# Attention stage of a streaming encoder layer: two key duplicates, one rope-key copy and the sums of the memory's squares are put in other slots

## The chip, the cores and the metric

One NeuronCore of a Trainium2 chip runs the kernel. The metric is the device time of one execution in microseconds (us). The kernel before took 849.5 us as the median of 3 runs (849.47 to 849.58).

## The reference, cut to what matters

One encoder layer is computed for 512 prompt tokens and 64 sample tokens (576 columns, `T`), float32. The input is normed and projected; two groups of 8 heads attend side by side; each group's output is normed, joined and projected by `w_o`; then come a cross-attention with 4 heads into 256 memory tokens, and a SwiGLU.

```python
h = rms_norm(x, g_mix)
fox_q, fox_k, fox_v, logf, mla_q, ckv, kr = project_mixers(h, pos, w_in, ...)
fox_o = attend(fox_q, fox_k, fox_v, ..., cum, cum)        # heads 0 to 7, keys of 64 rows
mk, mv = mla_keys_values(ckv, kr, w_ukv)                  # kr: the shared rope keys, 32 rows
mla_o = attend(mla_q, mk, mv, ...)                        # heads 8 to 15
x = x + concat(rms_norm(fox_o), rms_norm(mla_o)) @ w_o
m = rms_norm(mem, g_mem_src)                              # needs the sum of squares of each memory token
mem_k, mem_v = m @ w_mk, m @ w_mv
```

## The kernel before, in words

Each float32 product is made of three products of rounded parts (L460 to L462: high by high, low by high, high by low). ScalarE (ACT) rounds an operand to its high part; the low part is the rest, made by GpSimd (POOL) for weights, queries and keys and by VectorE (DVE) for activations. SyncE (SP) starts all loads.

The attention stage is one order written out by hand, in slots `s` from 0 to 96. There are 16 heads with 5 blocks of queries each, so 80 ticks; tick s is block s % 5 of head s // 5. In slot s, TensorE (PE) makes the scores of tick s (`scores`), then a piece of other work (`filler`, the slots in `CHUNKS`: a projection, a transpose of reciprocals, part of `w_o`), then the transposes of the probabilities of tick s - 2 (`turn`). DVE makes the maximum of tick s (`maxima`, L1666), evicts the filler of slot s - 1 (`evicted`, L1698 to L1743) and, in even slots, copies the transposed probabilities of tick s - 3 (`turned_dve`, L1676). ACT makes the exponentials of tick s (`expo`, L1044) and in odd slots the other copies. PE must not start a filler before the filler two before it is evicted (`filler_bank`: two PSUM banks in turn, semaphore `s_fev`), nor scores s before exponentials s - 2 (`s_ex`).

Dictionaries say what each engine does besides in which slot. Those the change touches: `KEY_HI_AT` (ACT: the high part of head c's keys, `key_hi`), `KEY_DUP_AT` (DVE: `key_dup`, L1640, a copy of 64 x 832 from the keys `kt` into the other half of `k1`), `KEY_LO_AT` (POOL: `key_lo`, L2155), `KR_AT` (POOL: the rope keys put under the keys of r, a copy L2199 and a rest L2201; first needed in slot 40), and `SPLIT_AT` (ACT: `split(b)`, the high part of weight block b; POOL's `rest(b)`, L2114, has its own `REST_AT`). Keys 6 are used from slot 30, keys 7 from slot 35. The pieces of all the dictionaries stand in one queue per engine, in the order in which the loop writes them.

For the memory, ACT squares `memf` (128 x 8 x 256) into `msq` in two halves in slots 71 and 73; POOL adds the halves up in slot 75 (L2212: 1024, 512 and 256 elements wide), and PE needs the sum in slot 87 (`s_mmacc`). From slot 75 on DVE makes the low parts of the memory (`meml`, L1797), after ACT made the high parts (`memh`).

Of the kernel before, what the change touches and what calls it, by code (L numbers as in the profile page):

```python
# [10 lines left out]
ALU = mybir.AluOpType  # L11
# [76 lines left out]
def build(nc, i_, o_, cum_dram):  # L88
# [10 lines left out]
    whi, c = place("whi", [128, 3, WB], F32R, c)  # L99
# [125 lines left out]
    with ExitStack() as ctx:  # L225
# [20 lines left out]
        def need(eng, s, value, i=0, per=0):  # L246

            if isinstance(i, int):
                if value + per * i > 0:
                    eng.wait_ge(s, value + per * i)  # L250
            else:
                eng.wait_ge(s, i * per + value)
# [787 lines left out]
        def _(act):  # L1040
# [137 lines left out]
            def high(j):  # L1178
# [10 lines left out]
                else:  # L1189
                    if j == 1:  # L1190
# [5 lines left out]

            HIGH_AT = (26, 31, 41, 51, 71, 77, 83, 89)
            QUERY_HI_AT = {1: 2, 2: 3, 9: 4, 10: 5, 19: 6, 20: 7}
            KEY_HI_AT = {5: 2, 6: 3, 14: 4, 15: 5, 25: 6, 28: 7}
            SPLIT_AT = {2: 16, 4: 17, 8: 18, 13: 19, 18: 20, 23: 21, 36: 22, 46: 23, 52: 24, 59: 25, 68: 26, 74: 27, 82: 28, 86: 29,  # L1200
                        87: 30, 92: 31, 93: 32}
            for s in range(LAST + 1):
                if 3 <= s < TICKS + 3 and s % 2 == 1:
                    turned_act(s - 3)
                if s - 1 in CHUNKS:
                    n = nth(s - 1)
                    bank = 6 + n % 2
                    for p, at in enumerate(KP_AT):
                        if s - 1 in (at, at + 1):
                            half = s - 1 - at  # L1210
                            act.wait_ge(s_fdone, n + 1)
                            if half == 0:
                                for r in (2 * p % 4, 2 * p % 4 + 1):
                                    act.wait_ge(s_qk, (5 * r + 25) if p < 2 else (5 * H + 5 * r + 5))
                            for e in range(2):
                                activation(keys_of(k1[2 * p % 4 + e][0:64, :], half), ps[64 * e:64 * e + 64, bank, 0:HK])\
                                    .then_inc(s_khi, 1)
                for h, at in enumerate(UQ_AT):
                    if s == at + 2:
                        act.wait_ge(s_fev, nth(at + 1) + 1)  # L1220
                        activation(q1[h % 4][:, :], qf[h % 4][:, :]).then_inc(s_uqhi, 1)
                if s < TICKS:
                    expo(s)
                if s in QUERY_HI_AT:
                    query_hi(QUERY_HI_AT[s])
                if s in KEY_HI_AT:
                    key_hi(KEY_HI_AT[s])
                if s in HIGH_AT:
                    high(HIGH_AT.index(s))
                if s in SPLIT_AT:  # L1230
                    split(SPLIT_AT[s])
                if s == FC_AT + 3:
                    act.wait_ge(s_fev, nth(FC_AT) + 1)
                    deviation(small[:, S_COL:S_COL + 5], small[:, S_COL:S_COL + 5], 512).then_inc(s_lsd, 1)
                if s == 70:
                    act.wait_ge(s_mem, 32)
                if s == 88:
                    act.wait_ge(n_col, 2)
                    deviation(small[:, S_MCOL:S_MCOL + 2], ps[:, 4, 0:2], D).then_inc(n_sd, 1)
                if s == 94:  # L1240
                    act.wait_ge(n_col, 3)
                    deviation(small[:, S_COL:S_COL + 5], ps[:, 4, 0:5], 512).then_inc(n_sd, 1)
                if s in (71, 73):
                    k = 4 * (s // 2 - 35)
                    act.wait_ge(s_qk, 70)
                    activation(msq[:, k:k + 4, :].rearrange("p a b -> p (a b)"), memf[:, k:k + 4, :].rearrange("p a b -> p (a b)"),
                               ACT.Square).then_inc(s_mmact, 1)
                if 74 <= s < 82:
                    k = s - 74
                    activation(memh[:, k, :], memf[:, k, :], scale=gains[:, G_SRC + k:G_SRC + k + 1]).then_inc(s_mmact, 1)  # L1250
# [245 lines left out]
        def _(dve):  # L1496
# [253 lines left out]
            LOW_AT = (27, 32, 42, 52, 72, 78, 84, 90)  # L1750
            QUERY_DUP_AT = {1: 2, 2: 3, 9: 4, 10: 5, 19: 6, 20: 7}
            MEMORY_LO_AT = (75, 76, 77, 80, 81, 82, 83, 84)
            KEY_DUP_AT = {5: 2, 6: 3, 14: 4, 15: 5, 25: 6, 28: 7}
            for s in range(LAST + 1):
                if s < TICKS:
                    maxima(s)
                if s - 1 in CHUNKS:
                    evicted(s - 1)
                if 3 <= s < TICKS + 3 and s % 2 == 0:
                    turned_dve(s - 3)  # L1760
                if 14 <= s <= 84 and s % 10 == 4:
                    joined(s // 10 - 1)
                if s % 10 == 0 and 10 <= s <= 80:
                    p = s // 10 - 1
                    dve.wait_ge(s_ex, 10 * p + 10)
                    need(dve, s_rb, p - 1)
                    at = S_SUM + 10 * (p % 2)
                    v.reciprocal(small[:, S_RI[p % 2]:S_RI[p % 2] + 10], small[:, at:at + 10]).then_inc(s_ri, 1)
                if s in QUERY_DUP_AT:
                    query_dup(QUERY_DUP_AT[s])  # L1770
                if s in KEY_DUP_AT:
                    key_dup(KEY_DUP_AT[s])
                if s in LOW_AT:
                    j = LOW_AT.index(s)
                    dve.wait_ge(s_ohi, j + 1)
                    dve.wait_ge(s_osq, j + 1)
                    v.scalar_tensor_tensor(hlo[:, j, :], out_of(j), gain(G_OUT, j), f(hhi[:, j, :]),
                                           ALU.mult, ALU.subtract).then_inc(s_olo, 1)
                if s == FC_AT + 5:
                    dve.wait_ge(s_lsd, 2)  # L1780
                    v.reciprocal(small[:, S_RCC:S_RCC + 5], small[:, S_COL:S_COL + 5]).then_inc(s_frc, 1)
                if s == 89:
                    dve.wait_ge(n_sd, 2)
                    v.reciprocal(small[:, S_MRC:S_MRC + 2], small[:, S_MCOL:S_MCOL + 2]).then_inc(n_rc, 1)
                if s == 91:
                    dve.wait_ge(n_row, 2)
                    v.tensor_copy(rmem[:, :], ps[:, 5, 0:NM]).then_inc(n_rs, 1)
                if s in (92, 93):
                    dve.wait_ge(n_rs, 2)
                    memory_key(s - 92)  # L1790
                if s == 95:
                    dve.wait_ge(n_sd, 3)
                    v.reciprocal(small[:, S_RCC:S_RCC + 5], small[:, S_COL:S_COL + 5]).then_inc(n_rc, 1)
                if s in MEMORY_LO_AT:
                    k = MEMORY_LO_AT.index(s)
                    dve.wait_ge(s_mmact, 2 + k + 1)
                    v.scalar_tensor_tensor(meml[:, k, :], memf[:, k, :], gain(G_SRC, k), f(memh[:, k, :]),  # L1797
                                           ALU.mult, ALU.subtract).then_inc(s_mmlo, 1)
# [308 lines left out]
        def _(pool):  # L2107
# [41 lines left out]
            def key_lo(c):  # L2149

                a = half_a(c)
                if c in (0, 2, 4, 6):
                    pool.wait_ge(f_lo, {0: 15, 2: 18, 4: 20, 6: 22}[c])
                pool.wait_ge(x_khi, c + 1)
                g.tensor_tensor(k2[c % 4][a, :], kt[a, :], f(k1[c % 4][a, :]), ALU.subtract).then_inc(x_klo, 1)  # L2155
                pool.wait_ge(x_klo, c + 1)
# [9 lines left out]
                       87: 30, 92: 31, 93: 32}  # L2166
            HIGH_AT = (26, 31, 41, 51, 71, 77, 83, 89)
            QUERY_LO_AT = {1: 2, 2: 3, 9: 4, 10: 5, 19: 6, 20: 7}
            KEY_LO_AT = {5: 2, 6: 3, 14: 4, 15: 5, 25: 6, 28: 7}
            RB_BUILD = (12, 26, 31, 41, 51, 70, 76, 82)  # L2170
            KR_AT = (27, 32, 37, 42)
            for s in range(LAST + 1):
                if s in RB_BUILD:
                    p = RB_BUILD.index(s)
# [15 lines left out]
                if s in KR_AT:  # L2190
# [1 line left out]
                    if r == 0:  # L2192
                        pool.wait_ge(s_kr, 4)
                    pool.wait_ge(s_qk, 5 * r + 25)
                    if r >= 2:
                        pool.wait_ge(s_uqlo, r)
                    else:
                        pool.wait_ge(s_rb, {0: 2, 1: 3}[r])
                    g.tensor_copy(k1[r][64:128, :], krf[64:128, :]).then_inc(s_krc, 1)  # L2199
                    pool.wait_ge(s_krc, 2 * r + 1)  # L2200
                    g.tensor_tensor(k2[r][64:128, :], krf[64:128, :], f(k1[r][64:128, :]), ALU.subtract).then_inc(s_krc, 1)  # L2201
# [1 line left out]
                if s - 1 in HIGH_AT and s not in (HIGH_AT[0] + 1, HIGH_AT[4] + 1):  # L2203
# [1 line left out]
                    pool.wait_ge(s_osq, j + 1)  # L2205
                    need(pool, s_oacc, j - 1 if j < 4 else j - 2)
                    g.tensor_tensor(sqacc[:, 0:T], sqacc[:, 0:T], tmp2[:, j % 2, :], ALU.add).then_inc(s_oacc, 1)
                if s == 75:
                    pool.wait_ge(s_mmact, 2)
                    for k, n in enumerate((4, 2, 1)):  # L2210
                        need(pool, s_mmacc, k)
                        g.tensor_tensor(msq[:, 0:n, :], msq[:, 0:n, :], msq[:, n:2 * n, :], ALU.add).then_inc(s_mmacc, 1)  # L2212

            def memory_key_lo(m):
                pool.wait_ge(s_mkhi, m + 1)
# [389 lines left out]
```

## Time and profile before

| what | us |
|---|---|
| median of 3 runs | 849.5 |
| profiled execution | 848.79 |
| its span in the trace | 847.0 |
| PE busy | 815.0 (96%) |
| DVE busy | 541.0 (64%) |
| ACT busy | 398.0 (47%) |
| POOL busy | 363.8 (43%) |

The span is the time from the first to the last instruction of the profiled execution; the 1.8 us around it belong to the launch. Busy time is the union of an engine's instructions, and PE's is modelled at its ends. The attention stage lies between about 95 and 306 us of the span.

### The profile page before, as it was taken

Reading aid. Unit: us, or ns where it says so; the run is one execution under the profiler, and the core shown is the slowest. Engines: PE = TensorE matmul, PEld = TensorE weight load, DVE = VectorE, ACT = ScalarE, POOL = GpSimd, SP = SyncE. Lnnn points to the kernel's source line nnn. Section 1 sums busy time; section 2 is a strip of 40 time slices with the busy share of each in tenths; the row PEclk is TensorE's granted clock in tenths of the full one; section 3 lists DMA queues with packets and bytes.
Section 4 is the critical chain, followed back from the end, with each engine's and each line's share of the span. In section 5 each row is a group of like instructions: output and inputs, shape, how many; then the busy total and the mean of one; then the engine's idle time right before and its main releaser. Section 6 shows DMA issues by size and latency. Waiting matters only on the chain.

```text
span 847.0 us, 16025 instructions
## 1 busy us (share of the span) xinstructions
PE 815.0 (96%) x5913; PEld 768.8 (91%) x5913; DVE 541.0 (64%) x911; ACT 398.0 (47%) x735; POOL 363.8 (43%) x213
## 2 busy tenths in 40 slices
PE   6999999999999999998999999999999989999995
PEld 6987998778887899987899999999999989999995
DVE  6245365666667755557488998889999887211214
ACT  6443464565676425455354555555455564221210
POOL 2652864555326444732195333333333335433420
PEclk9999999999999999999999999999999999999998
DMA  7332422201123333340041332222222223232103
GB/s 258 100 110 83 153 90 65 60 3 36 32 76 137 125 101 108 112 130 26 1 141 60 101 100 99 93 77 82 95 99 99 99 87 101 87 87 81 58 1 112
DMA packets 26391, 75.49 MB, mean 89 GB/s; under 512 B 3024, under 2 KB 7448, under 8 KB 26200
## 3 DMA queue, kind: packets, MB, share of 16 engines
q1 hardware_dynamic: 26336, 74.74, 27.7%
q8 instruction: 37, 0.61, 0.3%
q14 instruction: 18, 0.15, 0.1%
HBM read 68.20 MB, written 6.53 MB: 88 GB/s over the span
## 4 chain that ended last, share of the span: by engine, by line
PE 85%; DVE 7%; issue 2%; POOL 2%; ACT 2%; DMA 1%; DVEq 0%; SPq 0%; ACTq 0%
PE ps L460 26%; PE ps L462 25%; PE ps L461 25%; PE ps L612 2%; PE ps L630 2%; POOL hf L2241 1%; PE ps L874 1%; PE ps L478 1%; DVE tf L1914 1%; PE ps L591 1%; PE ps L590 1%; POOL wlo L2236 1%; PE ps L596 1%; DVE tl L1918 1%; PE ps L859 0%
## 5 line engine op out<-in xcount | busy, mean ns | idle before, releaser
L460 PE MATMUL ps<-hhi,whi 128*128 128x288 f32 x896 | 269.8, 301 | 11.9 <-DVE hlo L1519 6.9
L461 PE MATMUL ps<-hhi,wlo 128*128 128x288 f32 x896 | 265.7, 297 | 0.0
L462 PE MATMUL ps<-hlo,whi 128*128 128x288 f32 x800 | 237.5, 297 | 0.0
L2114 POOL TENSOR_TENSOR wlo<-wraw,whi 128x1024 fp32r<-128x1024 f32 (+1 forms) x48 | 113.5, 2369 | 174.7 <-ACT whi L1044 174.4
L460 PEld LDWEIGHTS ps<-hhi,whi 128*128 128x128 f32 x896 | 169.8, 190 | 15.1 <-issue 10.3
L1044 ACT ACTIVATE whi<-wraw 128x1024 fp32r<-128x1024 f32 (+3 forms) x138 | 114.7, 838 | 135.8 <-PE ps L462 121.7
L461 PEld LDWEIGHTS ps<-hhi,wlo 128*128 128x128 f32 x896 | 169.5, 189 | 0.2
L462 PEld LDWEIGHTS ps<-hlo,whi 128*128 128x128 f32 x800 | 151.2, 189 | 0.0
L2260 POOL TENSOR_TENSOR wlo<-wraw,whi 128x512 fp32r<-128x512 f32 x60 | 78.8, 1327 | 150.4 <-ACT whi L1044 150.4
L462 PE MATMUL ps<-hidlo,whi 128*128 128x288 f32 x352 | 104.7, 297 | 0.0
L2274 POOL TENSOR_TENSOR wlo<-wraw,whi 128x1024 fp32r<-128x1024 f32 (+1 forms) x24 | 56.3, 2348 | 79.6 <-ACT whi L1044 79.6
L1666 DVE TENSOR_REDUCE small<-ps 128x1 f32<-128x128 f32 (+4 forms) x80 | 39.0, 487 | 56.0 <-PE ps L596 50.9
L462 PE MATMUL ps<-tl,whi 128*128 128x288 f32 x240 | 71.4, 297 | 0.0
L461 PE MATMUL ps<-th,wlo 128*128 128x288 f32 x240 | 71.3, 297 | 0.0
L460 PE MATMUL ps<-th,whi 128*128 128x288 f32 x240 | 70.9, 295 | 0.0
L1044 ACT ACTIVATE whi<-ss 128x512 fp32r<-128x512 f32 x61 | 38.4, 631 | 63.6 <-PE ps L462 35.4
L462 PEld LDWEIGHTS ps<-hidlo,whi 128*128 128x128 f32 x352 | 66.7, 189 | 0.0
L1044 ACT ACTIVATE probs<-ps,small 128x128 f32<-128x128 f32 (+4 forms) x80 | 41.9, 524 | 42.8 <-DVE small L1666 42.0
L2064 DVE TENSOR_TENSOR tmp<-ps,rstd 128x576 f32<-128x576 f32 (+1 forms) x9 | 6.2, 691 | 85.2 <-PE ps L462 85.2
L460 PE MATMUL ps<-hidhi,whi 128*128 128x288 f32 x192 | 57.6, 300 | 2.1 <-DVE hidlo L2047 2.1
L461 PE MATMUL ps<-hidhi,wlo 128*128 128x288 f32 x192 | 57.4, 299 | 0.0
L460 PEld LDWEIGHTS ps<-th,whi 128*128 128x128 f32 x240 | 45.2, 188 | 0.0
(287 smaller groups left out, 1815.6 us busy)
## 6 DMA issues: line engine op xcount, KB each, us to landing
wraw<-w_ff SPq DMA_DIRECT2D x44, 512.0 KB, 4.1
wraw<-w_front SPq DMA_DIRECT2D x41, 512.0 KB, 3.6
wraw<-w_down SPq DMA_DIRECT2D x16, 512.0 KB, 3.7
wraw<-w_down SPq DMA_DIRECT2D x8, 384.0 KB, 3.1
wraw<-w_front SPq DMA_DIRECT2D x7, 384.0 KB, 3.4
xs<-x_t SPq DMA_DIRECT2D x8, 288.0 KB, 5.2
xa<-x_t SPq DMA_DIRECT2D x8, 288.0 KB, 4.7
out_y<-xb SPq DMA_DIRECT2D x16, 144.0 KB, 1.9
```

What stands on the lines that cost most here:

```text
L460: nc.tensor.matmul(out, lh, rh, start=start, stop=False)
L461: nc.tensor.matmul(out, ll, rh, start=False, stop=False)
L462: return nc.tensor.matmul(out, lh, rl, start=False, stop=stop)
L478: mm = nc.tensor.matmul(ps[:, bank, at + tt:at + tt + 1], source[:, 128 * tt:128 * tt + 128], ones[:, 0:1], start=True, stop=True)
L590: nc.tensor.matmul(out, q1[r][:, q], k1[r][:, ks], start=True, stop=False)
L612: mm = nc.tensor.transpose(ps[:, 2 + s % 2, 128 * kb:128 * kb + 128], probs[:, P_AT[u] + 128 * kb:P_AT[u] + 128 * kb + 128], ident[:, :])
L630: mm = nc.tensor.matmul(ps[64 * e:64 * e + 64, 4, 128 * kb:512], va[:, g, kb, h + e, :], pt[e][:, 512 * kb:512 * kb + 512 - 128 * kb], sta ...
L1044: return nc.scalar.activation(out, src, func, **kw)
L1666: v.tensor_reduce(nmax, ps[0:n, s % 2, 0:w], AX, ALU.max, negate=True).then_inc(s_mx, 1)
L2114: g.tensor_tensor(wlo[:, b % 3, 0:n], wraw[:, b % 2, 0:n], f(whi[:, b % 3, 0:n]), ALU.subtract).then_inc(f_lo, 1)
L2260: g.tensor_tensor(w_operand(1, j), src, f(w_operand(0, j)), ALU.subtract).then_inc(g_lo, 1)
L2274: g.tensor_tensor(ffw(n, 1, 1, w)[:, 0, :], (wraw2, wraw)[n % 4 // 2][:, n % 2, 0:w], f(ffw(n, 0, 1, w)[:, 0, :]), ALU.subtract).then_inc( ...
```

## The change

The duplicate of keys 6, with its high and low part, goes from slot 25 to slot 23, and the duplicate of keys 7 alone from 28 to 26. The first rope keys go from POOL's slot 27 to 30. The squares of the memory go from ACT's slots 71 and 73 to 70 and 71, block 27 is rounded by ACT in slot 73 in place of 74, and the three sums of the squares go from POOL's slot 75 to DVE's slots 72, 73 and 76. Some waits of POOL name other semaphores.

```diff
-            KEY_HI_AT = {5: 2, 6: 3, 14: 4, 15: 5, 25: 6, 28: 7}          # ACT
-            SPLIT_AT = {..., 68: 26, 74: 27, 82: 28, ...}
+            KEY_HI_AT = {5: 2, 6: 3, 14: 4, 15: 5, 23: 6, 28: 7}
+            SPLIT_AT = {..., 68: 26, 73: 27, 82: 28, ...}
...
-                if s in (71, 73):
-                    k = 4 * (s // 2 - 35)
+                if s in (70, 71):
+                    k = 4 * (s - 70)
                     act.wait_ge(s_qk, 70)
                     activation(msq[:, k:k + 4, :]..., memf[:, k:k + 4, :]..., ACT.Square).then_inc(s_mmact, 1)
...
-            KEY_DUP_AT = {5: 2, 6: 3, 14: 4, 15: 5, 25: 6, 28: 7}         # DVE
+            KEY_DUP_AT = {5: 2, 6: 3, 14: 4, 15: 5, 23: 6, 26: 7}
...
+                if s in (72, 73, 76):
+                    k = (72, 73, 76).index(s)
+                    n = 4 >> k
+                    dve.wait_ge(s_mmact, 2)
+                    need(dve, s_mmacc, k)
+                    v.tensor_tensor(msq[:, 0:n, :], msq[:, 0:n, :], msq[:, n:2 * n, :], ALU.add).then_inc(s_mmacc, 1)
...
-                if c in (0, 2, 4, 6):                                     # POOL, key_lo
-                    pool.wait_ge(f_lo, {0: 15, 2: 18, 4: 20, 6: 22}[c])
+                if c == 7:
+                    pool.wait_ge(s_rb, 2)
+                elif c % 2 == 0:
+                    pool.wait_ge(f_lo, {0: 15, 2: 18, 4: 20, 6: 21}[c])
...
-            KEY_LO_AT = {5: 2, 6: 3, 14: 4, 15: 5, 25: 6, 28: 7}
-            KR_AT = (27, 32, 37, 42)
+            KEY_LO_AT = {5: 2, 6: 3, 14: 4, 15: 5, 23: 6, 28: 7}
+            KR_AT = (30, 32, 37, 42)
...
-                    if r >= 2:
-                        pool.wait_ge(s_uqlo, r)
-                    else:
-                        pool.wait_ge(s_rb, {0: 2, 1: 3}[r])
+                    if r == 1:
+                        pool.wait_ge(s_rb, 3)
+                    else:
+                        pool.wait_ge(s_uqlo, max(r, 1))
...
-                if s == 75:
-                    pool.wait_ge(s_mmact, 2)
-                    for k, n in enumerate((4, 2, 1)):
-                        need(pool, s_mmacc, k)
-                        g.tensor_tensor(msq[:, 0:n, :], msq[:, 0:n, :], msq[:, n:2 * n, :], ALU.add).then_inc(s_mmacc, 1)
```

## Rows read from the trace of the kernel before

**Rows 1.** Busy time by stretch: PE, PEld, DVE, ACT, POOL; granted clock; DMA
```profile
160.00:170.00 10.00, 7.83 (x57) 6.68 (x57) 8.94 (x18) 7.37 (x19) 8.39 (x6) 1.00 0.36 100
...
260.00:270.00 10.00, 9.32 (x76) 8.11 (x77) 7.88 (x13) 6.16 (x16) 5.43 (x3) 1.00 0.60 223
270.00:280.00 10.00, 8.34 (x57) 6.71 (x57) 9.86 (x20) 7.04 (x16) 5.64 (x6) 1.00 0.42 153
```

**Rows 2.** PE in order of time, slots 29 and 30: start, us, idle before
```profile
167.25 0.22 PE L596 MATMUL ps<-maskb,identb 128*64 128x64 bf16 x1
...
170.63 0.45 PE L460 MATMUL ps<-ckvhi,whi 128*128 128x416 f32 x1 [2.29 <-DVE fo L1726]
```

**Rows 3.** DVE in order of time, slots 27 to 32
```profile
164.56 0.56 DVE L1666 TENSOR_REDUCE small<-ps 128x1 f32<-128x384 f32 x1 [0.61 <-PE ps L596]
...
167.41 2.05 DVE L1640 CAST k<-kt 64x832 fp32r<-64x832 f32 x1
169.38 0.48 DVE L1666 TENSOR_REDUCE small<-ps 64x1 f32<-64x320 f32 x1
169.89 0.69 DVE L1726 TENSOR_TENSOR fo<-fo,ps 128x512 f32<-128x512 f32 x1
...
177.86 0.81 DVE L1777 SCALAR_TENSOR_TENSOR hlo<-fo,gains,hhi 128x576 fp32r<-128x576 f32 x1
```

**Rows 4.** POOL in order of time, slots 23 to 27
```profile
159.83 1.84 POOL L2114 TENSOR_TENSOR wlo<-wraw,whi 128x768 fp32r<-128x768 f32 x1 [6.87 <-ACT whi L1044]
162.88 1.97 POOL L2155 TENSOR_TENSOR k<-kt,k 64x832 fp32r<-64x832 f32 x1 [1.22 <-ACT k L1044]
164.91 0.72 POOL L2178 COPY rb<-small 128x640 f32<-128x640 f32 x1
165.80 1.18 POOL L2199 CAST k<-krf 64x832 fp32r<-64x832 f32 x1 [0.17 <-POOL rb L2178]
167.06 1.95 POOL L2201 TENSOR_TENSOR k<-krf,k 64x832 fp32r<-64x832 f32 x1
```

**Rows 5.** All of one line: least, median, most ns, first and last start
```profile
L1640 DVE CAST k<-kt x8: 586/1314/2331, 97.6 to 167.4; 64x832 fp32r<-64x832 f32 x8
...
L1797 DVE SCALAR_TENSOR_TENSOR meml<-memf,gains,memh x8: 423/720/2316, 265.8 to 288.1; 128x256 fp32r<-128x256 f32 x8
```

**Rows 6.** PE in order of time, slots 76, 80 and 81
```profile
265.43 0.40 PE L460 MATMUL ps<-hhi,whi 128*128 128x288 f32 x1 [0.25 <-DVE olof L1726]
...
268.64 0.40 PE L460 MATMUL ps<-hhi,whi 128*128 128x288 f32 x1 [0.42 <-DVE olof L1726]
...
277.00 0.66 PE L707 MATMUL ps<-ident,rb 128*128 128x128 f32 x4 [0.81 <-DVE evt L1741]
...
278.92 0.52 PE L612 MATMUL ps<-ident,probs 128*128 128x128 f32 x3 [0.71 <-DVE pt L1676]
```

**Rows 7.** DVE in order of time, slots 72 to 77
```profile
258.81 0.81 DVE L1777 SCALAR_TENSOR_TENSOR hlo<-olof,gains,hhi 128x576 fp32r<-128x576 f32 x1
261.47 0.69 DVE L1666 TENSOR_REDUCE small<-ps 128x1 f32<-128x512 f32 x1 [1.85 <-PE ps L596]
...
262.97 0.48 DVE L1666 TENSOR_REDUCE small<-ps 64x1 f32<-64x320 f32 x1 [0.21 <-PE ps L462]
...
265.81 2.32 DVE L1797 SCALAR_TENSOR_TENSOR meml<-memf,gains,memh 128x256 fp32r<-128x256 f32 x1 [0.43 <-ACT memh L1044]
...
269.11 1.53 DVE L1797 SCALAR_TENSOR_TENSOR meml<-memf,gains,memh 128x256 fp32r<-128x256 f32 x1
```

**Rows 8.** POOL in order of time, slots 73 to 75
```profile
259.42 1.46 POOL L2189 TENSOR_TENSOR q<-qf,q 128x576 fp32r<-128x576 f32 x1 [2.93 <-ACT q L1044]
265.45 2.38 POOL L2114 TENSOR_TENSOR wlo<-wraw,whi 128x1024 fp32r<-128x1024 f32 x1 [4.57 <-ACT whi L1044]
267.80 4.89 POOL L2212 TENSOR_TENSOR msq<-msq 128x1024 f32<-128x1024 f32 x3
```

**Rows 9.** ACT in order of time, slot 73
```profile
262.88 1.05 ACT L1044 ACTIVATE msq<-memf 128x1024 f32<-128x1024 f32 x1
```

**Rows 10.** DVE groups by line and shape: busy, mean ns, idle before
```profile
L1954 DVE TENSOR_TENSOR wlo<-ss,whi 128x512 fp32r<-128x512 f32 x61 | 40.1, 684 | 0.0
...
L1918 DVE TENSOR_TENSOR hlo<-tf,hhi 128x1152 fp32r<-128x1152 f32 x1 | 1.4, 1359 | 0.0
```

More of the change, by code:

```diff
@@ L1198, in _ @@
             QUERY_HI_AT = {1: 2, 2: 3, 9: 4, 10: 5, 19: 6, 20: 7}
-            KEY_HI_AT = {5: 2, 6: 3, 14: 4, 15: 5, 25: 6, 28: 7}
-            SPLIT_AT = {2: 16, 4: 17, 8: 18, 13: 19, 18: 20, 23: 21, 36: 22, 46: 23, 52: 24, 59: 25, 68: 26, 74: 27, 82: 28, 86: 29,
+            KEY_HI_AT = {5: 2, 6: 3, 14: 4, 15: 5, 23: 6, 28: 7}
+            SPLIT_AT = {2: 16, 4: 17, 8: 18, 13: 19, 18: 20, 23: 21, 36: 22, 46: 23, 52: 24, 59: 25, 68: 26, 73: 27, 82: 28, 86: 29,
                         87: 30, 92: 31, 93: 32}
```

## The prediction

> **What bounds the kernel now.** I read the busy time by stretch first, then PE in order of time where it is not full, then the other engines around each gap. PE is busy 96% of the span, so only its gaps can be won. In the attention stage they lie in two places: 2.17 us between 160 and 170 us, and 0.68 + 1.66 = 2.34 us between 260 and 280 us, while the granted clock is full in all three stretches [rows 1]. These are the two places that the change touches.
>
> First place. In slot 30 PE stands 2.29 us in front of a filler, until DVE has evicted the filler of slot 28 [rows 2]. DVE is late because the duplicate of keys 7 took 2.05 us [rows 3], while the least of its eight took 0.586 [rows 5]. POOL's rest of the rope keys ran from 167.06 to 169.01 [rows 4], and the duplicate ended at 169.46, 0.45 us after it: it stood still until POOL was done, and then took about its own time. The maximum of tick 29 follows at 169.38, although PE had finished those scores at 167.25 + 0.22 = 167.47 [rows 2, 3].
>
> Second place. DVE is busy 9.86 of the 10 us from 270 to 280 [rows 1], and PE waits for it four times: 0.25, 0.42, 0.81 and 0.71 us, 2.19 in all [rows 6]. Some of DVE's work is again standing still beside POOL. The first two low parts of the memory take 2.32 and 1.53 us [rows 7], against 0.423 for the least of their kind [rows 5]. The first ends 0.30 us after POOL's `rest(27)` (265.45 + 2.38 = 267.83), the second inside POOL's three sums of squares [rows 8]. That is 1.90 + 1.11 = 3.0 us lost to POOL.
>
> **First place: duplicates and rope keys.** In slot 28 the duplicate leaves DVE. The maximum of tick 29 is then free to start when its scores are there: 167.47 + 0.04 (the lag between scores and maximum that other slots show) = 167.51, not 169.38, so 1.87 earlier. Its eviction L1726 starts 0.51 after it and PE 0.74 after that, as now [rows 2, 3]: 168.76 in place of 170.63. Of the 2.29 us PE still waits 0.42. **Gain 1.87 us.**
>
> What hides the moved pieces. The duplicate of keys 7 in slot 26 falls in front of the maximum of tick 27, where DVE idles 0.61 us [rows 3]; it takes 0.59 [rows 5], so nothing is left over, and nothing is late. POOL's order there becomes: low part of keys 6 (1.97) from the end of ACT's high part, about 159.75, to 161.8, then `rest(21)` (1.84) to 163.8, then the reciprocals (0.72) to 164.5 [rows 4]. The duplicate starts at about 163.9: just behind the last two-operand subtraction, beside a copy. If the copy holds it too, it is 0.5 us late; if `rest(21)` runs 1 or 2 us later, by up to 1.9. Nothing covers that: maximum 27, the query eviction behind it and the exponentials are what scores 29 wait for. So the place is worth between 0 and 2.0; I take 1.87, since the order leaves 0.1 us and the nearest neighbour is only a copy. ACT does the high part of keys 6 in slot 23 in front of `split(21)` and the exponentials of tick 24, 0.9 us later; PE asks for those in slot 26, about 1 us after their new end: nothing. `rest(21)` ends 2.1 us later, and the load behind it (block 23) is not needed before slot 46: nothing. DVE's duplicate of keys 6 goes between two instructions of slot 23 where it idles 0.68 us: nothing. Head 6 and 7 get their keys earlier than they need.
>
> The rope keys in slot 30. POOL now has a queue without a gap: low part of keys 7 from 168.6 (1.97 to 2.2), the rest of a query (1.46), rope keys 0 (1.18 + 1.95), reciprocals (0.72), rope keys 1 again 3.1, a sum [rows 4, 8]. It ends near 180.5; the next thing PE needs of it, the reciprocals for slot 36, are done by 176.1 and the rope keys well before slot 40. The one DVE instruction of that stretch with both operands in SBUF is the low part L1777, now at 177.86 [rows 3] and then 1.87 earlier, at 176.0: between the reciprocals (to 176.1) and the subtraction of rope keys 1 (177.1 to 179.1). If it meets the subtraction it stands up to 2 us, of which about 0.9 is covered. I take 0, and keep 1.1 as its bound.
>
> **Second place: the squares.** Times are those of before; all of it shifts with the first place. ACT squares in slots 70 and 71, where it idled 0.67 us and where nothing it delays is awaited; `split(27)` takes exactly the place of the second square, 262.88 to 263.93 [rows 9], so the exponentials around it stay and POOL's `rest(27)` goes from 265.45 to about 264.0, ending at 266.4.
>
> DVE gets three sums. The rows have no uncontended 1024 wide; 1152 wide takes 1.359 and 512 wide 0.684 [rows 10], so by the slope of 1.05 ns an element 1.22, 0.68 and 0.42 us: 2.3 in all, while POOL is rid of 4.89 [rows 8].
>
> Sum 1 starts at 258.81 + 0.81 = 259.6, in an idle of 1.85 us [rows 7]. POOL's query rest starts at 259.42 and ends at 260.88 [rows 8]; if DVE stands behind it, the sum ends at 260.88 + 1.1 = 262.0 and the maximum of tick 73 is 0.5 late; if not, at 260.8, and nothing is late. Sum 2 (0.68) stands in front of the maximum of tick 74, which idled 0.21 [rows 7]: 0.4 to 0.8 us late in all. The filler of slot 76, at 265.43 now [rows 6], starts that much later: up to 266.2.
>
> Then DVE gains. The first low part starts at 265.7 to 266.1 and ends 0.3 behind `rest(27)`: 266.7 to 267.1, not 268.13. Sum 3 (0.42) follows in slot 76, and the second low part takes 0.42 instead of 1.53 since POOL has no sums to make; by the second low part DVE is 1.7 us ahead of before (268.95 against 270.64). PE, in front of filler 77, finds the bank free; even by the later case it reaches filler 78 at 271.5, as now (271.52), and from there it is DVE's lead that counts: DVE comes to slots 78 to 80 between 1 and 2 us early (one collision of a residual sum with POOL stays, 0.4 to 0.8 us), more than the 0.81 and the 0.71 that PE waits for it [rows 6]. **Gain 0.81 + 0.71 = 1.5 us**, 1.8 if sum 1 does not stand. All of PE's gaps there are 2.2, the upper end; the lower end is a loss (third rival). I take 1.5, by the case in which the sum stands, as the duplicate in slot 28 did.
>
> The Trainium skill, page SBUF — State Buffer, section "SBUF: two separate sides", says that DVE and GpSimd share one pair of ports, that the one that starts first holds it for its whole instruction, and that a DVE instruction with two SBUF inputs takes part when the GpSimd one reads SBUF. The ends at 0.45 and 0.30 us after POOL's agree with it. By that rule sum 1 is the case that speaks against this change, and the gain of the place is 1.5, not 1.8.
>
> **Sum.** Profiled execution 848.79 - 1.87 - 1.5 = 845.4. The median of the runs stands 0.7 above the profiled execution, so 846.1. Behind slot 81 PE is full but for short waits on its own results, and its loads are started by the same chain, so nothing takes the gain back.
>
> **Rivals.**
> 1. Only the first place pays. The sums put 2.3 us on DVE where it is full 98% of the time, and what POOL no longer blocks is given back: sum 1 stands 1.3, and a residual sum meets POOL. For it: [rows 1, 7]. Against it: 3.0 us of standing still is more than the 1.1 us of sums 2 and 3. Time 849.5 - 1.9 = 847.6.
> 2. Only the second place pays. The duplicate in slot 26 stands behind `rest(21)`, or L1777 in slot 32 behind the rope keys, and 1 to 1.9 us come back as PE waits. For it: POOL's queue is without gaps at both, and the margin in slot 26 is 0.1 us. Against it: in slot 26 it takes POOL to be later than each of its durations says. Time 849.5 - 1.5 - 0 to 0.9 = 847.6.
> 3. Slower: sum 2 stands behind `rest(27)`. Place: DVE in slot 73. It decides from the point where sum 2 starts later than `rest(27)`, about 264.0; I have it at 262.7 to 263.2. Price: the sum then ends at 266.4 + 0.55 = 266.95, the maximum of tick 74 goes from 262.97 to 266.9, and filler 76 from 265.43 to about 269.0, so 3.6 us; if DVE stays the bound through slot 81 none of it comes back, and the time is 849.5 - 1.9 + 3.6 = 851.2. For it: ACT's `split(27)` is a slot earlier in the order. Against it: 0.8 us of margin, and PE's 1.9 us of later gaps would repay half.
>
> **How the numbers follow.** Forecast (both pay) 0.62; rival 1 0.15; rival 2 0.12; rival 3 0.06; something else, of either sign, 0.05. Time 846.1. The forecast's own spread is 845.1 (all gaps but 0.4 us go) to 847.1; rivals 1 and 2 lie at 847.6 and reach to 848.4; so 80% from 845.0 to 848.3. What a measurement of this kernel can tell from no change is about 0.2%, 1.7 us: faster are the forecast and most of rivals 1 and 2, together 0.80; within 0.2% 0.13; slower 0.07.
>
> **What would show it.** In the changed trace: PE's wait in slot 30 near 0.4 us and the duplicate of keys 7 near 0.6 us in front of the maximum of tick 27; L1777 of slot 32 at about 0.8 us; the sums at 1.2 (2.4 if it stands), 0.7 and 0.4 us; the second low part of the memory near 0.42; PE without the waits at slots 80 and 81. A duplicate of 1.5 us or more in slot 26, a sum 2 of 2 us or more, or PE waits in slots 76 to 81 still above 1.5 us in all would make the prediction wrong.

## The result, and the profile after

| | median us | lowest to highest | executions | ratio to before, 95% interval |
|---|---|---|---|---|
| before | 849.47 | 849.16 to 849.58 | 5 | |
| after | 844.85 | 844.24 to 846.02 | 5 | 0.9944, 0.9932 to 0.9956 |
| after, in two later comparisons | 845.92 and 846.15 | 844.07 to 847.44 | 6 and 6 | 0.9949 and 0.9951 |

The change makes the kernel 4.6 us faster (4.0 and 3.8 us in the later comparisons). The profiled execution of after took 844.98 us, its span is 843.2 us, its granted clock 0.992; before it was 848.79, 847.0 and 0.991.

**Where the time went.** The first sample-values matmul of a head pair (line 643) comes once in ten slots and makes a mark on PE. In the trace of after, PE in order of time, start and duration first:

```profile
157.03 0.57 PE L643 MATMUL ps<-pt,va 128*64 128x64 f32 x12
...
176.56 0.57 PE L643 MATMUL ps<-pt,va 128*64 128x64 f32 x12
...
259.42 0.57 PE L643 MATMUL ps<-pt,va 128*64 128x64 f32 x12
...
279.55 0.57 PE L643 MATMUL ps<-pt,va 128*64 128x64 f32 x12
```

In before the same marks stand at 157.34, 178.50, 261.36 and 283.46. The distances between them are the ruler for all that follows:

| us | start of slot 23 | 23 to 33 | 33 to 73 | 73 to 83 | 83 to the end | span |
|---|---|---|---|---|---|---|
| before | 157.34 | 21.16 | 82.86 | 22.10 | 563.54 | 847.0 |
| after | 157.03 | 19.53 | 82.86 | 20.13 | 563.65 | 843.2 |

The first place gave 1.63 us, the second 1.97; between them nothing changed. The change does not touch the start (0.31 us) and the end (0.11).

**First place.** PE of after in slots 29 and 30 (start, duration, and in brackets the idle time before it and what ended it):

```profile
166.87 0.36 PE L590 MATMUL ps<-k,q 128*64 128x320 f32 x1 [0.40 <-ACT probs L1044]
...
168.69 0.45 PE L460 MATMUL ps<-ckvhi,whi 128*128 128x416 f32 x1 [0.33 <-DVE fo L1726]
```

DVE of after, slots 27 to 32:

```profile
163.68 0.91 DVE L1640 CAST k<-kt 64x832 fp32r<-64x832 f32 x1
164.51 0.54 DVE L1666 TENSOR_REDUCE small<-ps 128x1 f32<-128x384 f32 x1
...
167.56 0.48 DVE L1666 TENSOR_REDUCE small<-ps 64x1 f32<-64x320 f32 x1 [0.17 <-PE ps L596]
167.97 0.67 DVE L1726 TENSOR_TENSOR fo<-fo,ps 128x512 f32<-128x512 f32 x1
...
175.92 0.81 DVE L1777 SCALAR_TENSOR_TENSOR hlo<-fo,gains,hhi 128x576 fp32r<-128x576 f32 x1
```

POOL of after, slots 23 to 26:

```profile
159.60 1.97 POOL L2163 TENSOR_TENSOR k<-kt,k 64x832 fp32r<-64x832 f32 x1 [6.95 <-ACT k L1044]
161.64 1.83 POOL L2120 TENSOR_TENSOR wlo<-wraw,whi 128x768 fp32r<-128x768 f32 x1
163.42 0.72 POOL L2186 COPY rb<-small 128x640 f32<-128x640 f32 x1
```

The wait of 2.29 us [rows 2] is 0.33, and the maximum of tick 29 follows its scores. The duplicate of keys 7 started 0.26 us after POOL's copy and ended at 164.59, 0.45 us behind the copy's end (164.14). The one in slot 28 had also ended 0.45 us behind a POOL instruction, a subtraction [rows 3, 4]. So a POOL copy holds it as well: it took 0.91 us, not 0.59, and in front of scores 29 PE waits 0.40 us, where before it waited 0.19 (at 166.81). Those 0.2 us are most of what the first place gave less than the forecast 1.87.

**Second place.** DVE of after, slots 72 to 77:

```profile
257.59 2.43 DVE L1799 TENSOR_TENSOR msq<-msq 128x1024 f32<-128x1024 f32 x1
...
261.14 0.68 DVE L1799 TENSOR_TENSOR msq<-msq 128x512 f32<-128x512 f32 x1
...
264.06 1.05 DVE L1803 SCALAR_TENSOR_TENSOR meml<-memf,gains,memh 128x256 fp32r<-128x256 f32 x1
...
266.10 0.41 DVE L1799 TENSOR_TENSOR msq<-msq 128x256 f32<-128x256 f32 x1
266.43 0.47 DVE L1803 SCALAR_TENSOR_TENSOR meml<-memf,gains,memh 128x256 fp32r<-128x256 f32 x1
```

POOL of after, slots 72 to 76:

```profile
257.48 1.46 POOL L2197 TENSOR_TENSOR q<-qf,q 128x576 fp32r<-128x576 f32 x1 [2.94 <-ACT q L1044]
262.46 2.37 POOL L2120 TENSOR_TENSOR wlo<-wraw,whi 128x1024 fp32r<-128x1024 f32 x1 [3.52 <-ACT whi L1044]
```

PE of after, its listed waits in slots 74 to 81:

```profile
261.28 0.66 PE L707 MATMUL ps<-ident,rb 128*128 128x128 f32 x4 [0.29 <-DVE rstd L1732]
...
264.19 0.40 PE L460 MATMUL ps<-hhi,whi 128*128 128x288 f32 x1 [0.31 <-DVE olof L1726]
...
275.02 0.52 PE L612 MATMUL ps<-ident,probs 128*128 128x128 f32 x3 [0.29 <-DVE pt L1676]
```

Sum 1 met POOL's rest of the query and stood behind it: POOL was done at 257.48 + 1.46 = 258.94, and the sum ended at 260.02, 1.08 us later. Sum 2 was well ahead of `rest(27)`, which started at 262.46. The first low part of the memory ended 0.28 us behind `rest(27)`, as in [rows 7, 8], but it had started late, so it lasts 1.05 and not 2.32 us; the second took 0.47, not 1.53. The waits of 0.42 and 0.81 us [rows 6] are gone, that of 0.71 is 0.29.

Busy time by stretch after (length, PE, PEld, DVE, ACT, POOL, granted clock, DMA):

```profile
160.00:170.00 10.00, 9.26 (x64) 7.99 (x65) 8.44 (x20) 7.80 (x22) 5.32 (x4) 1.00 0.30 92
260.00:270.00 10.00, 9.31 (x67) 8.11 (x68) 9.14 (x21) 7.34 (x19) 3.64 (x3) 1.00 0.43 167
270.00:280.00 10.00, 9.71 (x81) 7.88 (x79) 7.36 (x19) 6.14 (x13) 5.21 (x4) 1.00 0.45 159
```

Against [rows 1] PE won 1.43 us from 160 to 170, nothing from 260 to 270, and 1.37 from 270 to 280, where DVE fell from 9.86 to 7.36. The work has also moved up by 2 us there, so the marks, not these fixed windows, give the size.

### The profile page after: what moved, and what is told of

It reads as the page before. It is cut to its first block, busy times and chain, and to the rows that moved or that the text cites. A ratio compares the mean times of both kernels' runs of the same rounds, so it can differ in the third digit from the quotient of the medians.

```text
span 843.2 us, 16028 instructions
## 1 busy us (share of the span) xinstructions
PE 813.0 (96%) x5913; PEld 766.6 (91%) x5913; DVE 538.9 (64%) x914; ACT 397.9 (47%) x735; POOL 361.9 (43%) x210
## 4 chain that ended last, share of the span: by engine, by line
PE 82%; DVE 8%; ACT 3%; issue 3%; POOL 2%; DMA 1%; SPq 0%; DVEq 0%; ACTq 0%
PE ps L460 25%; PE ps L462 24%; PE ps L461 24%; PE ps L612 2%; PE ps L630 2%; POOL hf L2244 1%; PE ps L874 1%; PE ps L478 1%; ACT whi L1044 1%; DVE tf L1920 1%; PE ps L591 1%; PE ps L590 1%; DMA wraw<-w_front 1%; POOL wlo L2239 1%; ACT L1044 1%
## 5 line engine op out<-in xcount | busy, mean ns | idle before, releaser
L2120 POOL TENSOR_TENSOR wlo<-wraw,whi 128x1024 fp32r<-128x1024 f32 (+1 forms) x48 | 114.4, 2387 | 161.7 <-ACT whi L1044 161.3
L2277 POOL TENSOR_TENSOR wlo<-wraw,whi 128x1024 fp32r<-128x1024 f32 (+1 forms) x24 | 57.9, 2416 | 76.5 <-ACT whi L1044 76.5
```

What stands on the lines that cost most here:

```text
L2120: g.tensor_tensor(wlo[:, b % 3, 0:n], wraw[:, b % 2, 0:n], f(whi[:, b % 3, 0:n]), ALU.subtract).then_inc(f_lo, 1)
L2277: g.tensor_tensor(ffw(n, 1, 1, w)[:, 0, :], (wraw2, wraw)[n % 4 // 2][:, n % 2, 0:w], f(ffw(n, 0, 1, w)[:, 0, :]), ALU.subtract).then_inc( ...
```

## Experiments

The marks of each kernel, in us (e9 and e10 are told below); "wait" is PE's in front of the filler of slot 30, "clock" the mean clock granted from 171 to 176 us:

| kernel | 23 to 33 | 33 to 73 | 73 to 83 | 83 to the end | span | wait | clock |
|---|---|---|---|---|---|---|---|
| before, first profile | 21.16 | 82.86 | 22.10 | 563.54 | 847.0 | 2.29 | 1.00 |
| before, e11 | 22.78 | 82.85 | 22.08 | 562.98 | 848.3 | 2.30 | 0.66 |
| before, e12 | 22.75 | 82.87 | 22.11 | 562.34 | 847.3 | 2.29 | 0.66 |
| e2 sums only | 22.76 | 82.84 | 20.15 | 563.78 | 847.0 | 2.30 | 0.66 |
| e7 before, tiny sums | 22.54 | 82.86 | 20.71 | 562.68 | 846.4 | 2.29 | 0.71 |
| e14 before, 9 transposes | 21.18 | 82.88 | 22.10 | 565.40 | 848.5 | 1.32 | 1.00 |
| e13 before, 18 transposes | 21.19 | 82.90 | 22.08 | 564.13 | 848.2 | 0.34 | 1.00 |
| e1 first place only | 19.55 | 82.87 | 22.07 | 562.62 | 844.4 | 0.33 | 1.00 |
| e3 duplicate 7 only | 20.26 | 82.87 | 22.09 | 562.80 | 845.2 | none listed | 1.00 |
| e4 rope keys only | 19.70 | 82.87 | 22.10 | 562.44 | 844.3 | 0.82 | 1.00 |
| after, e5 | 19.53 | 82.87 | 20.13 | 563.93 | 844.3 | 0.33 | 1.00 |
| after, e16 | 19.53 | 82.86 | 20.14 | 565.45 | 845.4 | 0.32 | 1.00 |
| e6 after, tiny sums | 19.55 | 82.87 | 19.43 | 565.41 | 844.7 | 0.33 | 1.00 |
| e8 both wait | 19.30 | 82.88 | 19.72 | 562.65 | 842.7 | 0.33 | 1.00 |
| e15 both wait, again | 19.30 | 82.91 | 19.74 | 563.11 | 842.6 | 0.33 | 1.00 |

What lies behind slot 83 runs from 562.3 to 565.5 us with no relation to the edits. It follows the granted clock there: the time missing from full clock (length times the missing share, added up over stretches of 20 us) is 4.9 us in e12 and 5.0 in e4, the two shortest, and 8.9, 8.9 and 9.0 in e6, e14 and e16, the three longest. These falls hide 1 us in the times, but not in the marks.

### The two places, each by itself (e1, e2)

e1 is before with the edits of the keys and rope keys; e2 is after with just these taken back, so that only the squares are changed.

```diff
 e1, on before
-            KEY_DUP_AT = {5: 2, 6: 3, 14: 4, 15: 5, 25: 6, 28: 7}
+            KEY_DUP_AT = {5: 2, 6: 3, 14: 4, 15: 5, 23: 6, 26: 7}
-            KR_AT = (27, 32, 37, 42)
+            KR_AT = (30, 32, 37, 42)
...
 e2, on after: the reverse
```

> The kernel before with the first place alone changed (duplicates and low parts of keys 6 and 7, first rope keys); the squares and sums stay. Theory (additive, one shared port): PE's wait in slot 30 falls from 2.29 to about 0.33 us, scores 29 wait 0.2 us more, so 1.6 us of the 3.8 that the two traces differ by; 847.9 us. The second place looks as before (waits of 0.25, 0.42, 0.81, 0.71). Rival (the two places depend on each other): the gain at slot 30 is there but the second place moves too, so the time differs from 847.9 by more than 0.7.

> The kernel before with the second place alone changed (squares in ACT's slots 70 and 71, block 27 in slot 73, the three sums by DVE); the keys stay. Theory: PE's wait of 2.29 us in slot 30 stays, and from slot 73 to slot 82 PE comes 2.0 us earlier; 847.5 us. Sum 1 takes 2.4 us, the second low part of the memory 0.47. Rival (the forecast's own step, PE gains only its two listed waits): 1.5 us, 848.0.

Measured: e1 846.61 us (6 executions, ratio 0.9970, 0.9958 to 0.9982), e2 848.62 us (12, ratio 0.9984, 0.9973 to 0.9996), before beside them 849.44. By the marks e1 has all of the first gain (19.55) and nothing of the second (22.07), e2 the reverse (20.15). The places are independent and both pay: rivals 1 and 2 of the prediction are out. The times missed what was expected: e1 came 1.3 us under 847.9, by more than the 0.7 that its rival asked for, and e2 1.1 over 847.5 (its gain of 0.8 us has an interval from 0.3 to 2.3). Only the marks decide here. e2 shows something new: it has the slot-30 wait of before, and took 22.76 us from slot 23 to 33 where the first profile of before has 21.16.

### The duplicate against the rope keys (e3, e4)

```diff
 e3, on before
-            KEY_DUP_AT = {5: 2, 6: 3, 14: 4, 15: 5, 25: 6, 28: 7}
+            KEY_DUP_AT = {5: 2, 6: 3, 14: 4, 15: 5, 25: 6, 26: 7}
 e4, on before, with the waits of POOL that go with it
-            KR_AT = (27, 32, 37, 42)
+            KR_AT = (30, 32, 37, 42)
```

> The kernel before with one entry changed: DVE's duplicate of keys 7 in slot 26 in place of 28. Nothing moves on POOL, which does the low part of keys 6 from 162.9 to 164.85 us when DVE gets there at 163.9. Theory (the duplicate stands until POOL's instruction in progress ends, and ends 0.45 us after it): it lasts 1.4 us and ends at 165.3, the maximum of tick 27 is 0.7 us late, scores 29 wait 0.9 us more, gain about 1.0 us, 848.5. Rival (only its place in DVE's queue counts): it lasts 0.59, nothing is late, gain 1.9, 847.6.

> The kernel before with POOL's first rope keys in slot 30 in place of 27 and nothing else; the duplicate of keys 7 stays in DVE's slot 28. Theory (POOL's instruction is what made it slow): POOL is idle at 167.4 us, the duplicate takes 0.59 instead of 2.05, the maximum of tick 29 comes at 167.9, gain 1.4 us, 848.1. Rival (its place counts): it stays near 2 us, the gain is 0.

Measured: e3 847.70 us (9, ratio 0.9977, 0.9968 to 0.9987), e4 846.96 us (7, 0.9969, 0.9959 to 0.9980). DVE of e3:

```profile
163.82 1.32 DVE L1640 CAST k<-kt 64x832 fp32r<-64x832 f32 x1
166.02 1.36 DVE L1777 SCALAR_TENSOR_TENSOR hlo<-fo,gains,hhi 128x576 fp32r<-128x576 f32 x1
```

POOL of e3:

```profile
162.72 1.97 POOL L2155 TENSOR_TENSOR k<-kt,k 64x832 fp32r<-64x832 f32 x1 [1.22 <-ACT k L1044]
164.76 0.97 POOL L2178 COPY rb<-small 128x640 f32<-128x640 f32 x1
165.90 0.88 POOL L2199 CAST k<-krf 64x832 fp32r<-64x832 f32 x1 [0.17 <-PE ps L596]
```

Moved by itself, the duplicate stands again, behind the low part of keys 6 (to 164.69; it ends 0.45 later), and the low part L1777 at 166.02 stands beside the rope keys' cast (1.36 us, where the same instruction took 0.85 in e4). It still yields 0.90 us. In e4 the duplicate stayed in slot 28 with POOL idle and took 0.59 us, and PE waited 0.82. Either edit alone takes away PE's wait of 2.3 us; the duplicate's move adds only 0.15 us to what e4 gives (19.55 against 19.70). What cost the 2.05 us was not DVE's place in the order but POOL's work beside it: POOL's move alone gives 1.46 of the 1.61. By their medians e3 and e4 came 0.8 and 1.1 us under what was expected of the marks, as e1 did; e9 to e14 give a likely reason.

### What the sums cost on either engine (e5, e6, e7)

e5 is after, unchanged. e6 and e7 make the three sums one column wide on DVE (after) and on POOL (before), which leaves the sum of the memory's squares out.

```diff
-                    v.tensor_tensor(msq[:, 0:n, :], msq[:, 0:n, :], msq[:, n:2 * n, :], ALU.add)
+                    v.tensor_tensor(msq[:, 0:n, 0:1], msq[:, 0:n, 0:1], msq[:, n:2 * n, 0:1], ALU.add)
```

> The changed kernel itself once more, beside the kernel before. Two ways to make the forecast's time of the traces: theory (the profiled execution is one draw, so the distance of 0.7 us between it and the median of before is chance and must not be added): the change measures 3.8 to 4.6 us, about 845.3. Rival (the distance is fixed, runs without profile lie 0.7 above it for both kernels): 845.9 or more.

> The changed kernel with the three sums of DVE one column wide in place of 256 (the sum of squares is left out but for one column); same places and same waits. It prices the sums on DVE. Theory: sum 1 meets POOL only shortly and is 0.1 us long, maximum 73 and 74 are on time, PE comes 0.6 to 0.8 us earlier to slot 76, but of that only 0.3 us are left at slot 82, where the waits of the changed kernel sum to 0.9 in all; 0.3 to 0.9 us faster than the changed kernel. Rival (DVE is the bound through slot 81): 2 us or more faster.

> The kernel before with POOL's three sums one column wide (the sum of squares is left out but for one column). It prices what POOL's sums cost there through the shared port. Theory: the second and third low part of the memory take 0.42 to 0.5 us in place of 1.53 and 0.96, the first stays at 2.3 beside the weights' rest, DVE is 1.5 us ahead, PE gains 1.3 to 1.6 us, 848.1. Rival (POOL's sums cost nothing, the gain came from squares and block 27 being earlier): under 0.4 us.

Measured: e5 845.92 us (6, ratio 0.9949, 0.9936 to 0.9963), which by the time alone is what its rival said, e6 844.43 us (5, 0.9930, 0.9917 to 0.9943), e7 847.79 us (12, 0.9976, 0.9965 to 0.9986). Slots 73 to 83: POOL's sums cost 22.10 - 20.71 = 1.39 us before, DVE's still cost 20.13 - 19.43 = 0.70 after. The two tiny versions differ by another 1.28 (20.71 - 19.43). That is not the width of the sums but their place and the order around them, ACT's earlier squares and `rest(27)` among it; how it divides was not tried. Together 1.39 + 1.28 - 0.70 = 1.97. DVE of e6:

```profile
258.03 1.37 DVE L1799 TENSOR_TENSOR msq<-msq 128x4 f32<-128x4 f32 x1
...
261.17 0.15 DVE L1799 TENSOR_TENSOR msq<-msq 128x2 f32<-128x2 f32 x1
```

POOL of e6:

```profile
257.92 1.46 POOL L2197 TENSOR_TENSOR q<-qf,q 128x576 fp32r<-128x576 f32 x1 [2.95 <-ACT q L1044]
```

This is the cleanest reading of the stand in this study: an addition of 4 columns took 1.37 us, to 259.40, because POOL's rest of the query ran from 257.92 to 259.38; the next one, of 2 columns, took 0.15. An instruction that stands ends behind POOL's by 0.14 us less than it takes alone: this one 0.02 us behind, the low part of the memory 0.28 (0.42 alone), the duplicate 0.45 (0.59 alone), and sum 1 1.08 (1.22 alone, in e15 below).

### A better version (e8, e15, e16)

Two of the collisions can be avoided by order: POOL's reciprocals wait for the duplicate, its last query rest for sum 1.

```diff
                     pool.wait_ge(s_ri, p + 1)
+                    if p == 1:
+                        pool.wait_ge(x_kdup, 8)
...
                         pool.wait_ge(s_uqhi, h + 1)
+                        if h == 7:
+                            pool.wait_ge(s_mmacc, 1)
```

> The changed kernel with two more waits on POOL: its first reciprocals' copy of slot 26 waits until the duplicate of keys 7 is made, and its last query rest (slot 73) waits until sum 1 is made. Theory (a DVE instruction that meets POOL stands until POOL is done): the duplicate takes 0.59 in place of 0.91, sum 1 1.2 in place of 2.43, maximum 73 is 0.5 us and maximum 74 0.4 to 0.5 us earlier; 0.3 us gained in the first place and 0.3 to 0.6 in the second, so 0.5 to 0.9 us faster than the changed kernel. Rival (POOL's delayed query rest is now what scores 75 wait for, ending near the moment at which they start): no gain or a loss up to 0.5.

> The changed kernel with the two added waits of POOL again (reciprocals behind the duplicate of keys 7, rest of the last query behind sum 1). By the two places 0.65 us less than the changed kernel beside it, ratio to before about 0.9935; if what is gained there is lost behind slot 83, the same as the changed kernel.

> The changed kernel, unchanged, a third time: 844.8 to 845.9 us, ratio 0.994 to 0.995; slots 23 to 33 19.53 and 73 to 83 20.13 us.

Measured: e8 844.59 us (6, ratio 0.9941, 0.9929 to 0.9953), e15 844.51 us (6, 0.9933, 0.9919 to 0.9947), and beside e15 the changed kernel, e16, 846.15 us (6, 0.9951, 0.9937 to 0.9965), before 849.92. DVE of e15:

```profile
164.18 0.59 DVE L1640 CAST k<-kt 64x832 fp32r<-64x832 f32 x1
...
257.92 1.22 DVE L1799 TENSOR_TENSOR msq<-msq 128x1024 f32<-128x1024 f32 x1
```

Neither of them stands any more, and in two profiles each the marks give 0.23 + 0.40 = 0.63 us. By its median the version is 1.3 us (e8 against e5) and 1.6 us (e15 against e16) under the changed kernel beside it. What goes beyond 0.63 is not of the two places: in the profiles it lies behind slot 83, which the edit does not touch. Of the kernels that leave nothing out it is the fastest that ran.

### Why before is slower than its own first profile (e9 to e14)

The theory formed after e2: behind a wait of PE of 2.3 us (a stand, in short) the granted clock falls for a while, and the first profile of before is an execution in which it did not. e9 and e10 have after's orders, but the duplicate of keys 7 back in slot 28 and made 3 and 6 times, to vary the stand; e11 and e12 are before.

```diff
                 v.tensor_copy(k1[c % 4][half_b(c), :], kt[half_a(c), :])
+                for n in range(2 if c == 7 else 0):      # e10: 5
+                    v.tensor_copy(k1[c % 4][half_b(c), :], kt[half_a(c), :]).then_inc(x_gap, 1)
+                    dve.wait_ge(x_gap, n + 1)
```

> The changed kernel with DVE's duplicate of keys 7 back in slot 28 and made three times over, one behind the other, while POOL is idle: a gap of about 2.1 us in front of PE's filler in slot 30, made without any POOL instruction in the way. It tests what the clock does after such a gap, since two profiles of kernels with the 2.3 us gap show a granted clock of 0.57 and 0.72 in the 4 us behind it, and seven of kernels with 0.3 to 0.8 us show 1.00. Theory (the gap is enough, in a part of the executions): the gap costs 1.8 us always and 1.5 us more in some; median 1.8 to 3.3 over the changed kernel, single times in two groups 1.6 us apart. Rival (the lower clock there is chance and not tied to the gap): 1.8 us, one group.

> As before this one, with six copies: a gap of about 4 us. Theory (the gap is enough, and the longer the more surely): granted clock below 1.00 behind slot 30 in the profile, and nearly all executions at 3.7 + 1.5 = 5.2 us over the changed kernel, 850.5 or more. Rival (chance): 3.7 us over it, about 849.3, and a clock of 1.00 there.

> The kernel before, one more profile. Theory (the gap of 2.3 us lets the clock fall in some executions): either as in its first profile (clock 1.00 behind slot 30, 21.2 us from the sample values of slot 23 to those of slot 33) or 0.6 to 0.85 with 22.7 us; the distance of a single execution to its median is then no constant. Rival (a constant of 0.7 us by which runs without profile lie above it): 848.8 again.

> The same once more, with the same two answers; two further profiles of the kernel before say how often the lower clock comes behind slot 30 (2 of the 3 profiles with that gap so far).

Measured: e9 847.74 us (12, ratio 0.9978, 0.9966 to 0.9989), PE's wait 2.07 us, clock 0.69, slots 23 to 33 22.26 us; its single times lie evenly from 846.1 to 850.1 and not in the two groups that were expected. e10 853.26 us (7, 1.0038, 1.0024 to 1.0052), and its wait was 7.21 us, not 4: two of its copies stood behind POOL (the low part of keys 7 and the rope keys' cast) and took 2.21 and 1.15 us. Its clock was 0.55 from 171 to 176 us and 0.50, the 1.2 GHz level, from 176 to 180. e11 and e12 (850.16 and 849.14 us, one execution each) both show the fall that the first profile lacks. In e12 it reaches the 1.2 GHz level: each microsecond from 172 to 175 shows 0.50, so the 0.66 of the table is a mean of the two levels. PE of e12:

```profile
170.53 0.46 PE L460 MATMUL ps<-ckvhi,whi 128*128 128x416 f32 x1 [2.29 <-DVE fo L1726]
...
171.77 0.94 PE L612 MATMUL ps<-ident,probs 128*128 128x128 f32 x4
172.36 0.56 PE L590 MATMUL ps<-k,q 128*128 128x256 f32 x1
```

In the first profile the same transposes and scores took 0.60 and 0.36 us (at 171.87 and 172.22). None of these kernels parts PE's stand from what DVE and POOL do beside it. e13 and e14 settle it: before, with nothing earlier, but with idle work for PE in front of the filler.

```diff
+                if s == 30:
+                    pe.wait_ge(s_o, 2)
+                    for _ in range(18):      # e14: 9
+                        nc.tensor.transpose(ps[:, 5, 0:128], ident[:, :], ident[:, :])
                 filler(s)
```

> The kernel before, with 18 transposes of the identity (128x128) on PE in slot 30, in front of the filler that PE waits for, into a bank that nothing reads then: about 0.11 us each, 1.9 to 2.0 in all, so that PE is busy while DVE is as late as before. If PE's standing brings the lower clock: the wait of 2.29 us becomes about 0.3, the filler starts as late after the scores of slot 23 as before, the granted clock from 171 to 176 us is 1.00, slots 23 to 33 take 21.2 us instead of 22.75, and the time is about 1 us below before, though nothing is earlier. If the lower clock comes from something else (the power of all engines, chance): 0.66 to 0.70 in that stretch, 22.8 us, the time of before.

> The same with 9 transposes, 1.0 us of work and then a stand of about 1.3 us, a length that no kernel so far had. Theory (a stand of 2.1 us and more is followed by the lower clock, one of 0.8 not): it lies between, so this look says on which side 1.3 us falls: slots 23 to 33 take 21.2 us at a clock of 1.00, or up to 22.8. If something else brings the lower clock, e13 and e14 look alike.

PE of e13:

```profile
168.75 2.13 PE L749 MATMUL ps<-ident 128*128 128x128 f32 x18
171.22 0.46 PE L460 MATMUL ps<-ckvhi,whi 128*128 128x416 f32 x1 [0.34 <-DVE fo L1730]
```

Busy time by stretch in e12 (columns as above):

```profile
171.00:176.00 5.00, 5.00 (x24) 4.49 (x23) 1.99 (x5) 3.37 (x9) 4.71 (x5) 0.66 0.00 0
173.00:174.00 1.00, 1.00 (x5) 0.97 (x5) 0.58 (x2) 0.97 (x3) 0.87 (x2) 0.50 0.00 0
```

The same stretch in e13:

```profile
171.00:176.00 5.00, 4.79 (x29) 3.98 (x31) 3.24 (x9) 3.41 (x10) 4.71 (x5) 1.00 0.00 0
```

The same stretch in e14:

```profile
171.00:176.00 5.00, 5.00 (x33) 3.65 (x33) 2.29 (x6) 3.80 (x9) 4.79 (x4) 1.00 0.00 0
```

PE is busy for the whole stretch in e12 and in e14, but it starts 24 matmuls in the one and 33 in the other. e13 took 848.91 us (12 executions: 847.03 to 850.64, and one at 2773 that the ratio leaves out; ratio 0.9985, 0.9975 to 0.9995): idle work alone makes the kernel faster, by 1.3 us (0.4 to 2.1). e14, one execution, took 850.26, with 565.40 us behind slot 83. In both the filler starts as late as before (13.3 us behind the mark of slot 23 in e12, e13 and e14), the clock is 1.00, and slots 23 to 33 take 21.18 us. So it is PE's stand that brings the fall, and the fall costs 22.75 - 21.17 = 1.6 us (1.4 in e7). Of six profiles with a wait of 2.07 to 2.30 us five have it; of eleven with 1.32 us or less none. That rests on one profile each of e13 and e14 and on e13's shorter time; how often an execution of before has the fall, beyond two of its three profiles, was not measured.

## Why the prediction was right and wrong

**First place, 1.87 forecast, 1.63 measured.** The mechanism holds at each step: the stand behind POOL goes, the maximum follows its scores, PE waits 0.33 for a forecast 0.42. The step that was off is that the duplicate in slot 26 "takes 0.59, so nothing is left over, and nothing is late"; its own alternative, "if the copy holds it too, it is 0.5 us late", is what happened, at 0.3 us. L1777 met nothing: 175.92 and 0.81 us, for a forecast 176.0 and 0.8. The Trainium skill, page SBUF — State Buffer, section "SBUF: two separate sides", lets a GpSimd instruction hold the shared ports for its whole length against DVE's instructions in a two-port mode as well as those with two SBUF inputs. The prediction named only the latter, and the cast has one input; the 0.91 us behind a POOL copy and e15's 0.59 without one agree with the page if the cast runs in such a mode, which no trace here shows.

**Second place, 1.5 forecast, 1.97 measured.** Sum 1 stood behind the query rest (2.43 us, forecast about 2.4) and sums 2 and 3 took 0.68 and 0.41 (0.68 and 0.42). Against the scores of slot 73, filler 76 is 0.70 us later than before, forecast 0.4 to 0.8. The step that failed is "it reaches filler 78 at 271.5, as now": filler 77 is only 0.08 later, filler 78 0.27 earlier, the transposes of tick 77 0.51, filler 80 1.48 and the transposes of tick 79 1.96. Before, PE had more gaps of 0.1 to 0.3 us in slots 77 to 79 than the rows with a listed wait show, and DVE's lead took those too. The bound that was given, all 2.2 us of PE's gaps, held.

**The sum, 1.25 us too high.** In the profiled execution it gave 845.4 for 844.98. That this is so close is in part luck, since the errors cancel: the sum gave 0.47 too little in the second place and 0.24 too much in the first, and the profile came 0.31 earlier at slot 23 and 0.11 later behind slot 83, by chance. The other 0.83 us is the step that failed: "the median of the runs stands 0.7 above the profiled execution, so 846.1". The 0.7 was taken for a constant of the measurement, without a reason, and the lower end of the range, 845.0, carries it too. After the change the median stands 0.13 below the profiled execution, not 0.7 above.

What the runs show in its place is that this distance is no constant. It is +0.88 us in e4 and -2.06 in e6, two kernels without the stand, whose profiled stretches behind slot 83 are among the shortest and the longest (562.44 and 565.41). In the first profiles of before and after that stretch is nearly the same (563.54 and 563.65), so it does not explain why the one stands at +0.7 and the other at -0.13. What differs is the stand: the first profile of before lacked the fall of the clock that e11, e12, e2 and e7 show behind it, and the fall's price is twice the 0.7. The change removed the stand, and the fall with it. That this is the cause of the 0.83 is argued and not shown, since only one execution of each run has a trace. The sizes leave it open too: marks without the fall give a gain of 3.6 us, with it 5.2, and the three comparisons gave 4.6, 4.0 and 3.8, each known to about 1 us. The two later ones have the changed kernel at 845.92 and 846.15, almost on the forecast 846.1, but beside a before of 849.89 and 849.92; their gains are above the forecast 3.4 as well, and the agreement in time is luck.

One more reading was wrong, without effect on the sum: "Behind slot 81 PE is full but for short waits on its own results". In the trace of before PE waits there for DVE, up to 2.3 us at a time (line 1005). And no working in the prediction leads to the 848.4 to which rivals 1 and 2 are said to reach.

**Rivals.** The marks of e1 and e2 exclude 1 and 2. For rival 3, sum 2 was at 261.14 with `rest(27)` at 262.46: 1.3 us of margin where 0.8 was forecast.

## What to carry to other kernels

Take the gain of an edit from the wait it ends, but before carrying it from a profiled execution to a median, look at the granted clock behind that wait in more than one profile: a stand of TensorE can cost more than its own length, and filling it with idle work shows how much. Where a DVE instruction takes far more than the least of its kind and ends behind a POOL instruction by a little less than its own time alone, move POOL's, or make POOL wait for it. Distances between marks inside the trace resolve 0.1 us where medians of 5 to 12 executions do not resolve 1.

## What the runs showed of the hardware

- A TensorE stand of 2.07 to 2.30 us was followed, in five of six profiles, by a mean granted clock of 0.66 to 0.71 from 171 to 176 us (0.50, the 1.2 GHz level, for each microsecond from 172 to 175 in e12); matmuls with 416 columns then took 0.55 in place of 0.35 us (e9). After 7.21 us (e10) it was 0.50 for the stretch from 176 to 180. After 1.32 us or less, in eleven profiles, it stayed at 1.00; nothing was run between 1.32 and 2.07.
- A small DVE instruction stands for POOL as a large one does: 4 columns of addition took 1.37 us (e6). A maximum, which reads PSUM, did not: 128x256 took 0.41 us at 268.04 in before, inside POOL's first sum (267.80 to 270.35). A POOL copy of 128x640 with one input holds a DVE cast as its subtractions do (0.91 for 0.59 us).
- It goes the other way too: POOL's copy of the reciprocals took 0.97 us in e3, beside DVE's cast, and its rope subtraction 2.34, beside DVE's L1777 with operands in SBUF; before they took 0.72 and 1.95 [rows 4].
